# A ring of six weight slots for the dense layers, two expert slots given up for it, and the tokens loaded by another queue

## What is computed

```
# first block, layer 0
proj = x @ w_in                     # retention: 1024 x 6144
...
h = h + rms_norm(swiglu_ffn(...))   # 1024 x 5632 and 2816 x 1024
# layer 1: sparse attention, then an FFN of the same size
# second block
mod = jax.nn.silu(c) @ w_ada[l] + b_ada[l]          # 1024 x 6144
proj = h @ w_in[l]                                   # 1024 x 5632
...
g = jnp.einsum('becd,edf->becf', xe, w_gate)         # 16 x 1024 x 2048
u = jnp.einsum('becd,edf->becf', xe, w_up)           # 16 x 1024 x 2048
y = jnp.einsum('becf,efd->becd', jax.nn.silu(g) * u, w_down)   # 16 x 2048 x 1024
```

## Time and profile before

| what | value |
|---|---|
| median of 3 runs | 2339.54 us (2337.24 to 2343.74) |
| the profiled execution, its own time | 2333.71 us |
| its span in the trace | 2331.9 us |
| PE busy | 1778.3 us (76%) |
| DVE, ACT, POOL busy | 714.2, 576.1, 69.3 us |
| bytes read from HBM, mean rate | 594.45 MB, 257 GB/s |
| mean granted TensorE clock | 0.88 |

### The profile page before, as it was taken

How to read it: one execution, slowest core, us unless ns; L and a number is a source line. 1 busy time by engine, 2 the same in 40 slices (tenths; PEclk the granted TensorE clock), 3 DMA queues, 4 the chain that set the end, 5 groups by cost and what they waited for, 6 DMA issues and landing times.

```text
span 2331.9 us, 27317 instructions
## 1 busy us (share of the span) xinstructions
PE 1778.3 (76%) x11760; PEld 1217.7 (52%) x11760; DVE 714.2 (31%) x1133; ACT 576.1 (25%) x1016; POOL 69.3 (3%) x89
## 2 busy tenths in 40 slices
PE   5798789997998899979989766555666555556665
PEld 4667779996866799969946752111111111111111
DVE  2333454445366554455377430000000000000001
ACT  2234344443355434343354320000000000000000
POOL 0100010001000100010000100000000000000000
PEclk8899899998989999989989879888777887787877
DMA  7775564553701355533502329999999999999996
GB/s 179 262 281 216 189 207 163 180 181 100 225 1 55 108 181 180 176 131 127 178 3 92 144 113 425 427 428 428 427 429 428 427 428 428 428 427 429 427 427 263
DMA packets 160621, 603.29 MB, mean 259 GB/s; under 512 B 9542, under 2 KB 114151, under 8 KB 132711
## 3 DMA queue, kind: packets, MB, share of 16 engines
q1 hardware_dynamic: 146672, 586.18, 63.7%
q10 hardware_dynamic: 13848, 15.63, 3.1%
HBM read 594.45 MB, written 4.19 MB: 257 GB/s over the span
## 4 chain that ended last, share of the span: by engine, by line
PE 48%; DMA 41%; DVE 7%; ACT 2%; issue 1%; POOL 1%; ACTq 0%; DVEq 0%; SPq 0%
PE ps L608 19%; DMA late_expert_slots<-in_w_exp_down 12%; DMA late_expert_slots<-in_w_exp_gate 12%; PE ps L645 12%; DMA late_expert_slots<-in_w_exp_up 11%; DMA dense_ring<-in_ret_w_in 3%; PE ps L1090 3%; PE ps L632 2%; DVE split_operands L536 2%; PE ps L592 1%; PE ps L1111 1%; POOL residual L2011 1%; ACT split_operands L528 1%; PE ps L874 1%; DVE inv_root L1509 1%
## 5 line engine op out<-in xcount | busy, mean ns | idle before, releaser
L608 PE MATMUL ps<-split_operands 128*128 128x256 f32 x4128 | 516.5, 287 | 40.9 <-DVE split_operands L536 26.4
L608 PEld LDWEIGHTS ps<-split_operands 128*128 128x128 f32 x4128 | 509.4, 195 | 49.7 <-issue 46.4
L536 DVE TENSOR_TENSOR split_operands<-dense_ring,split_operands 128x1024 fp32r<-128x1024 f32 x194 | 233.0, 1243 | 297.9 <-ACT split_operands L528 297.9
L1979 DVE TENSOR_TENSOR arena<-arena,ps 128x512 f32<-128x512 f32 x16 | 11.0, 688 | 869.8 <-PE ps L1090 869.8
L528 ACT ACTIVATE split_operands<-dense_ring 128x1024 fp32r<-128x1024 f32 x194 | 194.2, 1050 | 234.7 <-DMA dense_ring<-in_ret_w_in 100.4
L1090 PE MATMUL ps<-late_expert_slots,arena 128*32 128x512 f32 x768 | 134.1, 836 | 101.0 <-DMA late_expert_slots<-in_w_exp_up 50.9
L645 PE MATMUL ps<-split_operands 128*128 128x256 f32 x1152 | 148.2, 294 | 28.6 <-DVE split_operands L546 18.2
L645 PEld LDWEIGHTS ps<-split_operands 128*128 128x128 f32 x1152 | 147.2, 203 | 30.1 <-issue 17.2
L536 DVE TENSOR_TENSOR split_operands<-dense_ring_tail,split_operands 128x1024 fp32r<-128x1024 f32 x94 | 111.0, 1222 | 157.3 <-ACT split_operands L528 157.3
L645 PE MATMUL ps<-hidden_split,split_operands 128*128 128x256 f32 x1056 | 133.4, 287 | 8.4 <-DVE split_operands L536 8.4
L645 PEld LDWEIGHTS ps<-hidden_split,split_operands 128*128 128x128 f32 x1056 | 131.2, 196 | 8.8 <-issue 8.8
(11 more groups left out here) (285 smaller groups left out, 1757.8 us busy)
## 6 DMA issues: line engine op xcount, KB each, us to landing
late_expert_slots<-in_w_exp_up SPq DMA_DIRECT2D x24, 2048.0 KB, 36.0
late_expert_slots<-in_w_exp_gate SPq DMA_DIRECT2D x24, 2048.0 KB, 36.1
late_expert_slots<-in_w_exp_down SPq DMA_DIRECT2D x24, 2048.0 KB, 35.8
expert_ring<-in_w_exp_gate SPq DMA_DIRECT2D x16, 2048.0 KB, 36.7
expert_ring<-in_w_exp_down SPq DMA_DIRECT2D x16, 2048.0 KB, 36.8
expert_ring<-in_w_exp_up SPq DMA_DIRECT2D x16, 2048.0 KB, 36.2
dense_ring_tail<-in_ffn_w_in SPq DMA_DIRECT2D x22, 1024.0 KB, 4.9
dense_ring<-in_ffn_w_in SPq DMA_DIRECT2D x22, 1024.0 KB, 5.0
```

Source lines behind the costliest of these rows:

```text
L536: dve.tensor_tensor(w_lo[:, n % 2, c], ring[U % RING][:, c], w_hi[:, n % 2, c], ALU.subtract).then_inc(lo_ready, 1)
L608: mm = pe.matmul(ps[:, bank, b * T:b * T + T], left, right, start=k == 0 and i == 0, stop=k == 7 and i == 2)
L1979: dve.tensor_tensor(e_hid, e_silu, ps[:, 5, :], ALU.mult).then_inc(e_hset, 1)
```

## The change

1. `RING` goes from 3 to 6. `expert_ring` and `dense_ring` become one tensor `dense_ring` of three times 2 MB, whose halves are the six slots.
2. `dense_ring_tail` becomes `dense_tables`: its first half is no longer a slot of the ring, its second half holds the small tables as before.
3. The eight expert slots are now: the piece of `arena`, `dense_tables`, the three parts of `dense_ring`, `late_expert_slots`. Loads 0 and 1 are no longer asked for in the retention's output. Load 0 waits for the second attention's scores, load 1 for its last product with the values (`s_pv`), loads 2, 3 and 4 for the splits of the last unit in each part of the ring. Loads 5 and later are as before.
4. The load of the tokens moves from ACT's queue to SP's, ahead of the first unit.

```
-RING = 3
+RING = 6
...
-        ering = sb("expert_ring", [P, 2, EUNIT])
-        ring_head = sb("dense_ring", [P, EUNIT])
-        ring_tail = sb("dense_ring_tail", [P, EUNIT])
+        ring_mem = sb("dense_ring", [P, 3, EUNIT])
+        ring_tail = sb("dense_tables", [P, EUNIT])
...
-        ring = [ring_head[:, 0:UNIT], ring_head[:, UNIT:2 * UNIT], ring_tail[:, 0:UNIT]]
+        ring = [ring_mem[:, i // 2, (i % 2) * UNIT:(i % 2) * UNIT + UNIT] for i in range(RING)]
...
-        e_slots = [ering[:, 0, :], ering[:, 1, :], arena_slot, ring_head[:], ring_tail[:]] +             [late_slots[:, i, :] for i in range(3)]
+        e_slots = [arena_slot, ring_tail[:]] + [ring_mem[:, i, :] for i in range(3)] + \
+            [late_slots[:, i, :] for i in range(3)]
...
+            sp.dma_start(h[:], a["xT"].rearrange("(k p) t -> p k t", p=P)).then_inc(x_in, 16)
...
-                if u in (3, 6):
-
-                    load_expert(u // 4)
...
-                if U0 == U_PA:
+                if U0 == U_PB:
 
                     sp.wait_ge(s_mm, 2 * HEADS)
-                    load_expert(2)
-            sp.wait_ge(lo_ready, 2 * SPLIT_NO[U_WO + 2] + 2)
-            load_expert(3)
-            sp.wait_ge(lo_ready, 2 * SPLIT_NO[U_WO + 3] + 2)
-            load_expert(4)
+                    load_expert(0)
+                    sp.wait_ge(s_pv, 2 * HEADS)
+                    load_expert(1)
+            for g, U in ((2, U_PB + 3), (3, U_WO + 1), (4, U_WO + 3)):
+                sp.wait_ge(lo_ready, 2 * SPLIT_NO[U] + 2)
+                load_expert(g)
...
-            act.dma_start(h[:], a["xT"].rearrange("(k p) t -> p k t", p=P)).then_inc(x_in, 16)
```

## The result

| | before | with the change |
|---|---|---|
| median of the runs | 2340.60 us (4 runs, 2337.24 to 2343.74) | 2305.12 us (4 runs, 2303.35 to 2306.31) |
| profiled execution, its span | 2333.71, 2331.9 | 2306.31, 2304.5 |

The ratio of the times is 0.9848, with a 95% interval from 0.9831 to 0.9865. The forecast was 2308.5, in a range of 2294 to 2323, so the change is faster, by 1.5%, and by about what was said: 35.5 us between the medians, 27.4 between the two profiled executions, where 31 was forecast. The two figures differ because the profiled execution of before lies 7 us under its median and that of after 1 us over its own. The sum by steps further down is made between the two profiled executions.

The account below looks back on a forecast made before the run. The prediction took the expert part as a DMA-full block of some 930 us behind the dense part. Dense savings 13 + 2 + 3.4 + 10.7 + 1.8 + 0 = 31 us gave 2339.5 - 31 = 2308.5 us, range 2294 to 2323.

Parts of the forecast that it names:

- start to pair 5: Start of the retention layer: four pairs before the stall instead of two, pair 5 earlier by 13 us (bounds 6 and 25).
- values: Values part of the retention layer: three waits of about 1.1 us for a split go, 3.4 us.
- gates: Retention gates: ACT splits a unit 5.5 us earlier, three PE waits and a half-clock slowdown go, 10.7 us (8 without slowdown).
- query product: Sparse attention: PE's wait for units of `nsa_w_in` goes, 1.8 us.
- The bound: Expert part: a block of some 930 us after the dense part, so each microsecond taken from the dense part comes off the end.
- The slower rival: Expert part: moved slots slow its stream; 3.5% less costs 32 us, at 5% the time is 2356; chance 0.03.
- no change: Whole kernel: needs a smaller start gain and unshrunk gates together and more, gain under 7 us; chance 0.03.
- The step that failed: Start: unit 6 is asked for at unit 0's split, 3 us ahead of the store, so pairs 0 to 3 have their units.
- this rival: Start gives less: bias table and store come later, unit 6 behind; gain 18 to 24; chance 0.22 shared with unshrunk gates.
- No stall behind the store: Start: queues take turns from the first packet, so no stall; gain 41 to 44 us, time 2295 to 2299; chance 0.08.
- The tokens: Start: their load moved to SP's queue, taken as 0; up to 1.5 us better or 3 worse.
- The expert requests: Retention's output and second attention: moving the expert loads' requests costs nothing, with a cover of over 30 us.

Follow-up runs that it names:

- run 2: The changed kernel with RING back at 3 slots, all other parts of the change kept: 2338.06 us, ratio 0.9992 to the kernel before.
- run 1: The changed kernel with the tokens' load back on ACT's queue: 2303.89 us, ratio 0.9845 to the kernel before.
- run 8: The changed kernel with the bias rows' store issued by POOL instead of ACT, at the same point: 2307.08 us, ratio 0.9855 to the kernel before.
- Run 9: The changed kernel with the bias rows made in and stored from 128 partitions, same bytes, queue and place: 2293.21 us, ratio 0.9800 to the kernel before.
- run 6: The changed kernel with expert loads 0 to 6 all asked for behind the last dense product: 2304.67 us, ratio 0.9853 to the kernel before.

## Why the prediction was right, and where it was not

The sum, between the two profiled executions:

| step | predicted | measured |
|---|---|---|
| start to pair 5 | 13 | 11.8 |
| pairs 5 to 8 | 2 | 2.0 |
| values | 3.4 | 4.7 |
| gates | 10.7 | 12.1 |
| output product and norms, up to the first FFN | 0 | -2.4 |
| query product | 1.8 | 3.0 |
| sparse attention | 0 | -4.7 |
| the rest of the dense part | 0 | 2.5 |
| expert part | 0 | -1.6 |
| sum (rounded) | 31 | 27.4 |

**The bound was read rightly.** What left the dense part left the total: slices of 427 to 429 GB/s in both, 934.3 us from the first expert to the end against 932.7. The slower rival (an expert stream slowed by its new slots) is out, and so is "no change".

**The step that failed** is one of the start: that unit 6 is asked for when unit 0 is split, "3 us ahead of the store", and so PE's wait comes "with four pairs done, not two". Unit 6 was asked for 2.4 us behind the store, and three pairs were done. I named as the danger that the table would come late and push the store back; it was the other way round. The tokens' move made the table come 6 us earlier and unit 0 land 9 us later (at 17.6). It was the tokens and not the six units at once: with three slots and the tokens on SP's queue (run 2) the bias matmuls start at 14.45 and unit 0 lands 16.8 us after its issue, with six slots and the tokens on ACT's (run 1) they start at 20.56 and unit 0 lands after 7.7. Before, the store hung on `bucket_cmp` through the bias matmuls and came 3 us behind DVE's split of unit 0; now both stand behind the late root (DVE splits the tokens first), and the store went first by 2.4 us. My sentence against this rival held that unit 0's split would not move; it moved, with unit 0's landing and with the root that ACT makes behind it. What the rival came to ("unit 6 is behind it") is what happened, though by an earlier store and a later unit 0 and not by the later table that it gave as its way, and run 1 shows that the forecast's mechanism is real when the tokens are left alone. That the term still came out at 11.8 beside 13 is luck, two errors against each other: PE had two pairs to do from the end of the stall to pair 5 (15.5 us) and not one (8.7), and the stall ended at 66.6, not at 72.3. For unit 6 behind the store I had priced a gain of 6 us, with pair 3 at 72. The unit that PE waits for is there some 35 us after the store's issue in both kernels (67.81 - 32.14 before, 64.17 - 29.04 now), and the store went out 3.1 us earlier; the 2 us that I added for another unit in front fell away, since unit 6 was itself the first behind the store.

**No stall behind the store** was the rival by the rule of turns. The stall stands at 12.8 us. Runs 8 and 9 show what it is. Its length is not a matter of which queue holds the store; it is that the store read from 16 partitions. From 16 it moves at 96 to 98 GB/s with the engines busy, on two different queues and with packets of two sizes; from 128 it moved at 257, and the two queues together at 339. The Trainium skill has a rule for that in "SBUF — State Buffer", section "Door 1: The DMA port swizzle": a transfer's rate goes by how many of SBUF's 16 ports its partitions reach, and partitions 0 to 15 reach four, measured there at 104 GB/s. The rates here, 96 to 98, are close to that. Run 9 changes the number of partitions, and with it how often each is read (16 times in place of 128); that it is the ports is the page's reading, which no run here takes apart. What it does to others the rows show: the loads to all 128 partitions behind the store moved 0.52 MB in 22 us. I had looked only at the queues' packets and took the standstill for a matter of order; 1279 packets at 98 GB/s with the engines 91% busy already said that each transfer was slow.

**The other terms.** The three waits of the gates went, and the values' with them; the values gave 1.3 us more than priced and the gates 1.4. Most of this stands in rows of before that I had not counted, the product L683, for which PE waited for ACT, and the L676 behind it:

```profile
123.48 0.66 PE L683 MATMUL ps<-tabs,dense_ring_tail 128*128 128x128 f32 x4 [0.98 <-ACT dense_ring_tail L1175]
...
183.49 0.66 PE L683 MATMUL ps<-tabs,dense_ring_tail 128*128 128x128 f32 x4 [0.47 <-ACT dense_ring_tail L1175]
...
185.18 1.07 PE L676 MATMUL ps<-dense_ring,cond_silu 128*32 128x512 f32 x8 [1.03 <-DVE mod L1543]
```

With the change the same product (L682) has no wait at either place, and the third wait is 0.44 us. That is 1.0 us of the values' part and 1.1 of the gates'. The query product gave 3.0 instead of 1.8: its wait of 1.8 went, and the KV product ahead of it took 36.58 us instead of the 37.78 of before, for the same 288 matmuls: before, PE ran at half clock from the product's start at 562.9 until about 569, and with the change only from 534.8 to about 537. That is no work of the ring. The tokens were worth nothing by run 1, as forecast, though by two effects that cancel. The expert requests cost nothing by run 6.

**What was lost** lies where PE ran at half clock longer. In the sparse attention before, and then after:

```profile
652.00:673.00 21.00, 18.30 (x57) 11.59 (x58) 13.84 (x54) 9.87 (x46) 0.00 (x0) 0.53 0.00 0
```

```profile
620.00:652.00 32.00, 28.48 (x87) 17.71 (x88) 19.67 (x74) 14.09 (x65) 0.00 (x0) 0.52 0.00 0
```

Columns: stretch, its length, busy time and count of PE, PEld, DVE, ACT, POOL, granted clock, DMA share, GB/s. Before, some 21 us of this attention ran at half clock (1.2 GHz), after some 31. In both the clock falls as PE goes idle for 3.8 us at the same place (before at 651, after at 620), and rises again under work. In the profiles of the ten runs it lasts 19 us once (run 6) and 27 to 38 in the others, the longest in run 2, whose time is that of before. The attention's own time goes with it: from L814 (after's L813) to its output product it is 116.6 us before, 121.3 after, and again 116.6 in run 6, a kernel with six slots, and 122.9 in run 2 with three. The start and the end of the attention in run 6:

```profile
597.18 0.46 PE L804 MATMUL ps<-tabs,arena 60*128 60x60 f32 x4
...
713.80 25.63 PE L635 MATMUL ps<-split_operands 128*128 128x256 f32 x192 [5.70 <-DVE split_operands L536]
```

So the length changes from execution to execution; that of before was a short one, in an execution 7 us under its median. The 4.7 us are therefore no effect of the six slots; what sets the length stays open. The output product's 1.1 us (48.66 against 47.53) is of the same kind: its first 5 us were at half clock with the change, its first 2.6 before.

## What to carry to other kernels

Ask of a store how many partitions it reads from before asking what stands behind it: one of 3 MB from 16 partitions held the DMA engines at some 100 GB/s for about 30 us, on either of two queues, and with the same bytes from 128 the kernel was as fast as with the store moved away (2293.2 and 2293.0). A deeper ring gains twice, by hiding slots that come free late and by putting work ahead of such a stall; to know which, run it once without the stall (here 17 of 33 us were left by the times, 21 of 30 by the start of the output product). And where an engine works in its written order, a load that is brought forward can delay another behind it, and the step behind the late one: the tokens brought forward gave nothing as long as the root stood behind unit 0's split, and with the root ahead of it the kernel was 7.9 us faster.

## What had not been expected of the hardware

- The first loads share the DMA unevenly. With the tokens ahead of the units on SP's queue, the tokens landed 5.9 us after issue (11.9 from ACT's queue before), and unit 0, next in the same queue, 16.4 us after issue (7.9 before), while ACT's `bucket_cmp` came 6 us earlier. Three or six units behind the tokens made no difference to it (16.8 in run 2). The loads of one queue landed in their order, but one more transfer ahead of unit 0 made it 8 to 9 us later.
- Packets three times as large did not make the 16-partition store faster: 96 GB/s from POOL's queue, 97 to 98 from ACT's.
- The half-clock stretch in the same sparse attention lasted about 20 us in two profiled executions and 27 to 38 in ten others; between before and after it made 4.7 us.
